# Attention's probabilities turned in 32x32 blocks by VectorE and put in place by DMA from SP's queue, instead of turned by TensorE; ten fillers at the beginning instead of eight

## Chip, cores, metric

The kernel runs on one core of a Trainium2 chip. The metric is the device time in microseconds of one execution. The version before took 2187.5 us (median of three runs, 2187.41 to 2187.93).

## What is computed

One decoder layer over 256 tokens of width 2048: a SwiGLU block with hidden width 5632, a mixer, a second SwiGLU block, each followed by a residual and a LayerNorm. The mixer projects the tokens by w_in, runs attention in nine pieces, gates the results and multiplies by two branch matrices and w_o. The change touches the part between scores and values:

```
proj = h @ w_in                                  # q, k, v of all branches, and the gates
# for each branch and group of four heads:
s = einsum('bhqd,bhkd->bhqk', q, k) * scale
p = exp(where(mask, s, -inf) - max)              # divided by its sum later
o = einsum('bhqk,bhkd->bhqd', p, v)
...
merged = sigmoid(g_a) * (o_nsa @ w_branch_a) + sigmoid(g_b) * (o_dil @ w_branch_b)
mix = merged @ w_o
```

Queries lie along the partitions after the scores. The values' product contracts over the keys, so the probabilities must be turned: keys along the partitions.

## The kernel before

**Weights in slots.** Every weight matrix goes through the core in 776 slots of two 128-row blocks by 512 columns (512 KB). SP loads a slot into one of four buffers `raw` (`load_slot`, L491), ScalarE rounds it to `w_hi` (`round_slot`, L519), VectorE writes the remainder `w_lo` (`split_slot`, L526), TensorE multiplies (`multiply_slot`): eight 128x512 matmuls with `w_hi` (L536, L537) and four with `w_lo` (L542). `w_hi` and `w_lo` have four buffers each too. SP may load a slot once the slot four before it is split, and ScalarE may round it once TensorE has used the slot four before it.

**The mixer's order.** The mixer has 192 slots (`MIX_SEQ`). Slots 32 to 79 are a mixture: behind each two slots of w_in stands one slot of the compression's weights (`cmp_slot`), which has two matmuls with `w_hi` (L1955) and two with `w_lo` (L1958) only, so it is short. Every third slot from 34 to 79 is such, slots 58, 61, 64 and 76 among them. `plan()` gives each small task of attention a slot behind which TensorE does it: turning queries and keys (`qT`, `kT`), scores (`s`, L1852, L1856, L1847), turning probabilities (`pT`, L1874), values (`pv`, L1905). ScalarE and VectorE take a task's result out of its PSUM bank two slots later in their own order (`LAG`). All engines' orders are written out from this table.

**Nine units.** `UNITS` 0 to 3 are selected and window attention of the two groups, 4 and 5 the compressed one, 6 to 8 the three dilated patterns. Units 0 to 3 and 6 have three blocks of 512 columns (four heads by 128 keys), units 7 and 8 two: 19 blocks in seven units. Each block is turned by four transposes on TensorE (`probs_T`, L1874, a matmul with the identity) into a PSUM bank, and VectorE copies it to `pT` (L1532). Before the scores of unit u+1 are masked into the same buffers (`mask_scores`, L1319), VectorE waits until TensorE has turned unit u's last block.

**Where the units stand.** In unit 0 the turns are at slots 58 to 60, the next scores at 61 to 63, the values at 65 and 66; in unit 1 at 71 to 73, 74 to 76, and 78 and 79.

**A form of the same technique** is there already: in both SwiGLU blocks the hidden activations are turned in 32x32 blocks by VectorE (`turn_blocks`, L1096), and 16 DMAs of ScalarE's queue put the blocks in place in `hT_lo` (`place_h`, L725), 256 pieces of 128 bytes each.

**The beginning.** Before the first weights are there, TensorE does `WARM_START` matmuls of zeros (`keep_warm`, L1642), then the first chunk (L1664, L1667, L1671).

Of the kernel before, what the change touches and what calls it, by code (L numbers as in the profile page):

```python
# [23 lines left out]
F32 = mybir.dt.float32  # L24
# [5 lines left out]
P = 128  # L30
# [17 lines left out]
WARM_START = 8  # L48
# [85 lines left out]
class Plan:  # L134


    def __init__(self):
        self.k, self.uses, self.t, self.at, self.by_pos = 1, [1, 1, 0, 0], {}, {}, {}
        self.turn = list(range(BANKS))

# [8 lines left out]
def plan():  # L149
# [36 lines left out]
    for u, (kind, g, ready) in enumerate(UNITS):  # L186
# [15 lines left out]
        n_probs = n_blocks(u)  # L202
        earliest = max(scored + 8, pv_read - 1)
        for j in range(n_probs):
            earliest = place(("pT", u, j), earliest)
        probs_read = earliest
        earliest += 5
# [51 lines left out]
def build(nc, x, xT_c, vec_c, w1_gate, w1_up, w1_down, ln1_g, ln1_b, w_in, ck_w2, cv_w2, ckv_w1,  # L259
# [9 lines left out]
    with ctx:  # L269
# [70 lines left out]
        s0 = sb("s0", [P, HPG, P])  # L340
        s1 = sb("s1", [P, HPG, TOKENS])
# [3 lines left out]
        pT = sb("pT", [P, 3, HPG, P])  # L345
# [68 lines left out]
        h_split = sem("h_split")  # L414
        var_ready = sem("var_ready")
# [286 lines left out]
        def exponentials(act, u, heads):  # L702
# [8 lines left out]
            for e in heads:  # L711
                v = s0[:, e] if e < HPG else s1[:, e - HPG, 0:P] if by_class(u) else s1[:, e - HPG]
                nc.scalar.activation(v, v, ACT.Exp, bias=negmax[:, u, e:e + 1], scale=SCALE,  # L713
                                     accum_out=sums[:, u, e:e + 1]).then_inc(probs_ready, 1)

        def place_h(act, f, i, n):
# [3 lines left out]
            for v in range(2 * (n - PLACE_FROM), 2 * (n - PLACE_FROM) + 2):  # L720
# [4 lines left out]
                act.dma_start(dst, src).then_inc(h_placed[f], 16)  # L725

# [12 lines left out]
        def _(sp):  # L739
# [311 lines left out]
        def _(dve):  # L1051
# [242 lines left out]
            def mask_scores(name, t):  # L1294
# [4 lines left out]
                if u:  # L1299
                    last = max(T[("pT", u - 1, jj)].k for jj in range(n_blocks(u - 1)))  # L1300
                    dve.wait_ge(bank_filled, last + 1)
                m = 0 if kind != DIL else 1 + g
# [4 lines left out]
                elif by_class(u):  # L1307
                    src = bank[:, t.bank, :].rearrange("p (h n) -> p h n", h=HPG)
                    dst = s0[:, :, :] if j == 0 else s1[:, :, 0:P]
# [11 lines left out]
            def maxima(u):  # L1321
# [10 lines left out]
                link(nc.vector.tensor_reduce(negmax[:, u, HPG:2 * HPG], s1[:, :, 0:P] if by_class(u) else s1[:, :, :], AX_X, ALU.max))  # L1332
                nc.vector.tensor_scalar(negmax[:, u, :], negmax[:, u, :], -SCALE, None, ALU.mult).then_inc(max_ready, 1)  # L1333

# [123 lines left out]
            for pos in range(MIX_SLOTS):  # L1458
# [56 lines left out]
                for name in pl.by_pos.get(pos - LAG, ()):  # L1515
# [3 lines left out]
                    elif name[0] == "pT":  # L1519
# [4 lines left out]
                        if UNITS[u][0] == CMP:  # L1524
                            n = HPG * N_CMP
                            hi, lo = pT_cmp[0:n, j, :], pT_cmp[V_ROW:V_ROW + n, j, :]
                            link(nc.vector.memset(pT_cmp[V_ROW // 2:V_ROW, j, :].bitcast(F32), 0.0))
                            link(nc.vector.tensor_copy(hi, bank[0:n, t.bank, 0:P]))
                            nc.vector.tensor_tensor(lo, bank[0:n, t.bank, 0:P], hi.bitcast(F32), ALU.subtract) \
                                .then_inc(bank_emptied[t.bank], 1)  # L1530
                        else:
                            nc.vector.tensor_copy(pT[:, j], bank[:, t.bank, :].rearrange("p (h n) -> p h n", h=HPG)) \  # L1532
                                .then_inc(bank_emptied[t.bank], 1)
# [16 lines left out]
                if pos in max_at:  # L1550
                    maxima(max_at[pos])
                if pos - 2 in max_at and UNITS[max_at[pos - 2]][0] == CMP:
# [69 lines left out]
        def _(pe):  # L1622
# [237 lines left out]
            def probs_T(name, t):  # L1860
# [4 lines left out]
                if UNITS[u][0] == CMP:  # L1865
                    n = HPG * N_CMP
                    mm = nc.tensor.transpose(bank[0:n, t.bank, 0:P], s0[:, 0, 0:TILES * HPG * N_CMP][:, j * n:(j + 1) * n], ident)
                else:
                    for h in range(HPG):
                        if by_class(u):  # L1870
                            v = s1[:, h, 0:P] if j else s0[:, h, :]
                        else:
# [196 lines left out]
```

## Time and profile before

| | |
|---|---|
| median of three runs | 2187.5 us |
| profiled execution, its own time | 2188.59 us |
| its span, first to last instruction | 2186.8 us |
| mean granted TensorE clock | 0.998 |
| TensorE busy | 2174.1 us, 99% of the span |
| VectorE busy | 1265.2 us, 58% |
| ScalarE busy | 964.6 us, 44% |
| DMA queue 1 (SP's), share of 16 engines | 63.2% |
| mixer's slots 30 to 190 in the trace | about 817 to 1294 us |

A row of a timeline gives start and duration in us, the engine, line, operation, tiles written and read, and how often it is repeated; in brackets, idle time before it and what ended it. PE is TensorE, DVE VectorE, ACT ScalarE; SPq and ACTq are DMAs issued by SP and ScalarE. Ends of matmuls are modelled, so the distance between two starts is what one costs. A 128x128 matmul in float32 shows as two records.

### The profile page before, as it was taken

What the parts mean: (1) busy time and instruction counts of PE and PEld (TensorE: products, weight loads), DVE (VectorE), ACT (ScalarE), POOL (GpSimd) and SP (SyncE); (2) the same over time, 40 slices, a digit from 0 to 9 for tenths busy, and PEclk for the clock granted to TensorE, in tenths of its full rate; (3) what the DMA queues carried; (4) which work ended last, traced back from release to release, by engine and by line L of the source; (5) the groups of instructions that cost most, each with busy time, mean ns of one, the idle gap of its engine ahead of it and who ended that gap; (6) DMA issues with size and microseconds to landing.
All of it is one profiled execution on the core that took longest, in us unless ns stands there. A gap on an engine that the chain in (4) does not pass through costs nothing.

```text
span 2186.8 us, 26659 instructions
## 1 busy us (share of the span) xinstructions
PE 2174.1 (99%) x9852; PEld 1801.2 (82%) x9852; DVE 1265.2 (58%) x1238; ACT 964.6 (44%) x1097; POOL 7.7 (0%) x12
## 2 busy tenths in 40 slices
PE   9999999999999999999999999999999999999998
PEld 8888888888888888888888888888888888888886
DVE  5555555554444767776655646567555555555445
ACT  5444444444333645544354444464444444444332
POOL 0000000000000000000000000000000000000000
PEclk9999999999999999999999999999999999999999
DMA  8767676777566666756567576656767676776664
GB/s 291 217 194 214 193 218 191 218 233 210 194 193 193 179 197 194 218 166 171 157 181 202 166 222 200 191 167 201 216 196 217 191 216 198 212 244 195 193 193 139
DMA packets 316203, 436.50 MB, mean 200 GB/s; under 512 B 112096, under 2 KB 112864, under 8 KB 315104
## 3 DMA queue, kind: packets, MB, share of 16 engines
q1 hardware_dynamic: 220096, 423.38, 63.2%
q10 hardware_dynamic: 96032, 12.08, 3.5%
q8 instruction: 51, 0.84, 0.2%
q14 instruction: 24, 0.20, 0.0%
HBM read 420.18 MB, written 3.68 MB: 194 GB/s over the span
## 4 chain that ended last, share of the span: by engine, by line
PE 99%; DVE 0%; ACT 0%; DMA 0%; DVEq 0%; issue 0%
PE acc L536 31%; PE acc L537 31%; PE acc L542 31%; PE bank L1905 1%; PE acc L1664 1%; PE acc L1667 1%; PE acc L1671 1%; PE bank L575 0%; PE bank L1745 0%; PE bank L1852 0%; PE bank L1874 0%; PE bank L1958 0%; PE bank L1955 0%; PE bank L1856 0%; PE bank L1847 0%; PE bank L1631 0%
## 5 line engine op out<-in xcount | busy, mean ns | idle before, releaser
L526 DVE TENSOR_TENSOR w_lo<-raw,w_hi 128x1024 fp32r<-128x1024 f32 x768 | 931.9, 1224 | 621.9 <-ACT w_hi L519 618.5
L519 ACT ACTIVATE w_hi<-raw 128x1024 fp32r<-128x1024 f32 x766 | 805.5, 1059 | 911.0 <-PE acc L542 815.6
L536 PE MATMUL acc<-w_hi,act_hi 128*128 128x512 f32 x2160 | 851.6, 394 | 0.0
L537 PE MATMUL acc<-w_hi,act_lo 128*128 128x512 f32 x2160 | 842.4, 390 | 0.0
L542 PE MATMUL acc<-w_lo,act_hi 128*128 128x512 f32 x2160 | 579.6, 390 | 0.0
L542 PEld LDWEIGHTS acc<-w_lo,act_hi 128*128 128x128 f32 x2160 | 405.5, 188 | 85.5 <-DVE w_lo L526 0.9
L536 PEld LDWEIGHTS acc<-w_hi,act_hi 128*128 128x128 f32 x2160 | 405.8, 188 | 83.8 <-issue 1.0
L537 PEld LDWEIGHTS acc<-w_hi,act_lo 128*128 128x128 f32 x2160 | 406.2, 188 | 81.6
L537 PE MATMUL acc<-w_hi,hT_lo 128*128 128x512 f32 x688 | 267.9, 389 | 0.0
L536 PE MATMUL acc<-w_hi,hT_hi 128*128 128x512 f32 x688 | 267.9, 389 | 0.0
L542 PE MATMUL acc<-w_lo,hT_hi 128*128 128x512 f32 x688 | 185.2, 389 | 0.0
L537 PEld LDWEIGHTS acc<-w_hi,hT_lo 128*128 128x128 f32 x688 | 129.3, 188 | 26.7
L542 PEld LDWEIGHTS acc<-w_lo,hT_hi 128*128 128x128 f32 x688 | 129.2, 188 | 26.7
L536 PEld LDWEIGHTS acc<-w_hi,hT_hi 128*128 128x128 f32 x688 | 129.2, 188 | 26.7
L1083 DVE SCALAR_TENSOR_TENSOR gate_t<-gate_t,acc 128x1024 f32<-128x1024 f32 x22 | 26.9, 1222 | 91.7 <-ACT gate_t L868 91.7
L868 ACT ACTIVATE gate_t<-acc 128x1024 f32<-128x1024 f32 x22 | 22.6, 1028 | 95.0 <-PE acc L542 90.6
L1091 DVE TENSOR_TENSOR gate_t<-gate_t,acc 128x1024 f32<-128x1024 f32 x22 | 26.9, 1222 | 62.0 <-PE acc L542 59.4
L536 PE MATMUL acc<-w_hi,oT_hi 128*128 128x512 f32 x96 | 38.0, 396 | 0.0
L537 PE MATMUL acc<-w_hi,oT_lo 128*128 128x512 f32 x96 | 37.5, 390 | 0.0
L713 ACT ACTIVATE s<-s,negmax 128x128 f32<-128x128 f32 (+1 forms) x56 | 23.8, 428 | 20.3 <-DVE negmax L1333 20.3
L696 ACT ACTIVATE qT<-bank 128x512 f32<-128x512 f32 x14 | 10.4, 743 | 42.8 <-PE bank L1745 42.8
L1096 DVE STREAM_TRANSPOSE hid<-gate_t 128x1024 f32<-128x1024 f32 x22 | 27.3, 1239 | 0.0
(241 smaller groups left out, 866.1 us busy)
## 6 DMA issues: line engine op xcount, KB each, us to landing
raw<-in_ffn_w_down_dram SPq DMA_DIRECT2D x176, 512.0 KB, 4.6
raw<-in_w_in_dram SPq DMA_DIRECT2D x176, 512.0 KB, 3.9
raw<-in_ffn_w_gate_dram SPq DMA_DIRECT2D x175, 512.0 KB, 4.5
raw<-in_ffn_w_up_dram SPq DMA_DIRECT2D x175, 512.0 KB, 4.5
raw<-in_w_o_dram SPq DMA_DIRECT2D x32, 512.0 KB, 4.7
hT_lo<-hid ACTq DMA_DIRECT2D x352, 32.0 KB, 3.5
raw<-in_cmp_kv_w_dram SPq DMA_DIRECT2D x16, 512.0 KB, 4.1
raw<-in_w_branch_a_dram SPq DMA_DIRECT2D x16, 512.0 KB, 5.3
```

The costliest lines, as they stand in the source:

```text
L519: nc.scalar.activation(weights(n0, s if isinstance(i, int) and i == 0 else s + per)[0], raw[:, r, :], ACT.Copy).then_inc(hi_done, 1)
L526: nc.vector.tensor_tensor(lo, raw[:, r, :], hi.bitcast(F32), ALU.subtract).then_inc(lo_done, 1)
L536: nc.tensor.matmul(o, a_hi[:, kt0 + k, at], hi, start=first and k == 0, stop=False)
L537: nc.tensor.matmul(o, a_lo[:, kt0 + k, at], hi, start=False, stop=False)
L542: mm = nc.tensor.matmul(o, a_hi[:, kt0 + k, at], lo, start=False, stop=last and k == SLOT_KT - 1)
L713: nc.scalar.activation(v, v, ACT.Exp, bias=negmax[:, u, e:e + 1], scale=SCALE, accum_out=sums[:, u, e:e + 1]).then_inc(probs_ready, 1)
L868: nc.scalar.activation(gate_t[:, :, :], acc_pair(0), ACT.Tanh, scale=0.5).then_inc(gate_tanh, 1)
L1083: nc.vector.scalar_tensor_tensor(gate_t[:, :, :], gate_t[:, :, :], 1.0, acc_pair(0), ALU.add, ALU.mult).then_inc(acc_emptied[0], 1)
L1091: nc.vector.tensor_tensor(gate_t[:, :, :], gate_t[:, :, :], acc_pair(1), ALU.mult).then_inc(acc_emptied[1], 1)
L1096: nc.vector.transpose(hid_kt.rearrange("p k t n -> p t k n"), gate_t[:, :, :].rearrange("p t (k n) -> p t k n", n=P)) \
L1664: nc.tensor.matmul(o, act_hi[:, 2 * s + k, at], hi, start=s == 0 and k == 0, stop=False)
L1667: nc.tensor.matmul(o, act_lo[:, 2 * s + k, at], hi, start=False, stop=False)
```

## The change

- `s0` and `s1` become parts of one tile `probs`, 12 blocks of 128 columns (8 used in units 7 and 8). `pT` gets the same form.
- For the seven units that are not compressed, `pT` tasks leave TensorE's table. VectorE turns `probs` in place in two instructions (`turn_probs`), at the slots `pl.turned[u]` (56, 68, 80, 92, 130, 142, 154) and the one behind.
- SP issues 16 DMAs per unit (`place_probs`), four behind each of the loads of slots turned+7 to turned+10. Each moves 32 partitions by 12 (or 8) pieces of 128 bytes from `probs` to `pT`.
- VectorE's first mask of the next unit waits until all 16 have landed, and so does TensorE's first values task (at turned+8). With that, in unit 0 the next scores stay at slots 61 to 63 and the values stand at 64 and 65; in unit 1 the scores stand at 73 to 75 and the values at 76 and 77. Later tasks shift by up to four slots.
- `WARM_START` goes from 8 to 10.

```diff
-WARM_START = 8
+WARM_START = 10
...
+        else:
+            pl.turned[u] = max(scored + (6 if u == 0 else 5), pv_read)
+            probs_read = pl.turned[u] + 6
+            earliest = pl.turned[u] + 8
...
-        s0 = sb("s0", [P, HPG, P])
-        s1 = sb("s1", [P, HPG, TOKENS])
+        probs = sb("probs", [P, 3 * HPG, P])
+        s0 = probs[:, 0:HPG]
+        s1 = probs[:, HPG:].rearrange("p (h j) n -> p h (j n)", h=HPG)
...
+        def place_probs(eng, u, moves):
+
+            eng.wait_ge(probs_turned, 2 * turned_to(u))
+            if u:
+                wait_filled(eng, T[("pv", u - 1, 1)])
+            n = HPG * (2 if by_class(u) else 3)
+            for v in moves:
+                b, q = divmod(v, QUADS)
+                src = probs[QUAD * b:QUAD * b + QUAD, 0:n].rearrange("p m (q j) -> p m q j", q=QUADS)[:, :, q, :]
+                dst = pT[QUAD * q:QUAD * q + QUAD, 0:n].rearrange("p m (b j) -> p m b j", b=QUADS)[:, :, b, :]
+                eng.dma_start(dst, src).then_inc(probs_placed, 16)
...
             for pos in range(MIX_SLOTS + TAIL_SLOTS):
                 load_slot(sp, mix_src[pos], mix_slot, 0, 0, pos)
+                for u in turned_units:
+                    k = pos - pl.turned[u] - 3 - RING
+                    if 0 <= k < 4:
+                        place_probs(sp, u, range(4 * k, 4 * k + 4))
...
                 wait_filled(dve, t)
-                if u:
+                if u and UNITS[u - 1][0] == CMP:
                     last = max(T[("pT", u - 1, jj)].k for jj in range(n_blocks(u - 1)))
                     dve.wait_ge(bank_filled, last + 1)
+                elif u:
+                    wait_placed(dve, u - 1)
...
+            def turn_probs(u, half):
+
+                dve.wait_ge(probs_ready, exps_before[u + 1])
+                n = HPG if by_class(u) else 6
+                v = probs[:, n * half:n * half + n].rearrange("p m n -> p (m n)")
+                nc.vector.transpose(v, v).then_inc(probs_turned, 1)
...
                 pe.wait_ge(probs_ready, exps_before[u + 1])
                 wait_bank_free(pe, t)
-                if UNITS[u][0] == CMP:
-                    n = HPG * N_CMP
-                    mm = nc.tensor.transpose(bank[0:n, t.bank, 0:P], s0[:, 0, 0:TILES * HPG * N_CMP][:, j * n:(j + 1) * n], ident)
-                else:
-                    for h in range(HPG):
-                        if by_class(u):
-                            v = s1[:, h, 0:P] if j else s0[:, h, :]
-                        else:
-                            v = s1[:, h, j * P:(j + 1) * P] if j < 2 else s0[:, h, :]
-                        mm = nc.tensor.transpose(bank[:, t.bank, h * P:(h + 1) * P], v, ident)
...
-                for j in range(n_blocks(u)):
-                    wait_moved(pe, T[("pT", u, j)])
+                if kind == CMP:
+                    for j in range(n_blocks(u)):
+                        wait_moved(pe, T[("pT", u, j)])
+                else:
+                    wait_placed(pe, u)
```

The order on VectorE around unit 0, before. L526 is a split; L1412 to L1420 work on keys and queries of a finished chunk; L1532 copies a turned block; L1319 masks a block of unit 1's scores.

```order
L526 TENSOR_TENSOR w_lo<-raw,w_hi 128x1024
L1417 TENSOR_TENSOR chunks_lo<-acc,rope 128x1024
L526 TENSOR_TENSOR w_lo<-raw,w_hi 128x1024
L1420 TENSOR_TENSOR chunks_lo<-chunks_lo,rot_tmp 128x1024
L526 TENSOR_TENSOR w_lo<-raw,w_hi 128x1024 x2
L1532 COPY pT<-bank 128x512
L526 TENSOR_TENSOR w_lo<-raw,w_hi 128x1024
L1532 COPY pT<-bank 128x512
L526 TENSOR_TENSOR w_lo<-raw,w_hi 128x1024
L1532 COPY pT<-bank 128x512
L526 TENSOR_TENSOR w_lo<-raw,w_hi 128x1024
L1319 TENSOR_TENSOR s<-bank,masks 128x512
```

The same place now (L535 is the split, L1378 a turn, L1357 the mask):

```order
L1378 STREAM_TRANSPOSE probs<-probs 128x768
L535 TENSOR_TENSOR w_lo<-raw,w_hi 128x1024
L1462 TENSOR_TENSOR chunks_lo<-acc,rope 128x1024
L1378 STREAM_TRANSPOSE probs<-probs 128x768
L535 TENSOR_TENSOR w_lo<-raw,w_hi 128x1024
L1465 TENSOR_TENSOR chunks_lo<-chunks_lo,rot_tmp 128x1024
L535 TENSOR_TENSOR w_lo<-raw,w_hi 128x1024 x5
L1357 TENSOR_TENSOR probs<-bank,masks 128x512
L535 TENSOR_TENSOR w_lo<-raw,w_hi 128x1024
L1357 TENSOR_TENSOR probs<-bank,masks 128x512
```

The three copies between the splits are gone, two turns stand among the splits of slots 56 to 58, and the first mask stands behind five splits in a row.

The order on SP at the same unit, now; before, only the loads stand here. L500 is a load of weights, L757 the moves.

```order
L500 DMA raw<-in_w_in_dram 128x2x512 x2
L757 DMA pT<-probs 32x12x32 x4
L500 DMA raw<-in_cmp_kv_w_dram 128x2x512
L757 DMA pT<-probs 32x12x32 x4
L500 DMA raw<-in_w_in_dram 128x2x512
L757 DMA pT<-probs 32x12x32 x4
L500 DMA raw<-in_w_in_dram 128x2x512
L757 DMA pT<-probs 32x12x32 x4
L500 DMA raw<-in_cmp_kv_w_dram 128x2x512
```

Behind each of the loads of slots 63 to 66 stand four moves; the load of slot 67 follows the last.

## Rows read from the trace of the kernel before

**Rows 1.** The page, part 1: busy us, share of the span, instructions
```profile
PE 2174.1 (99%) x9852; PEld 1801.2 (82%) x9852; DVE 1265.2 (58%) x1238; ACT 964.6 (44%) x1097; POOL 7.7 (0%) x12
```
**Rows 2.** The page, part 4: chain that ended last, by engine
```profile
PE 99%; DVE 0%; ACT 0%; DMA 0%; DVEq 0%; issue 0%
```
**Rows 3.** Timeline of TensorE, 918 to 925 us: two slots and two turned blocks
```profile
918.45 0.39 PE L536 MATMUL acc<-w_hi,act_hi 128*128 128x512 f32 x1
...
921.18 0.60 PE L1874 MATMUL bank<-small,s 128*128 128x128 f32 x4
921.54 0.48 PE L536 MATMUL acc<-w_hi,act_hi 128*128 128x512 f32 x1
...
924.39 0.60 PE L1874 MATMUL bank<-small,s 128*128 128x128 f32 x4
```
**Rows 4.** VectorE's groups by line: count, busy us, mean ns, idle before and releaser
```profile
L526 DVE TENSOR_TENSOR w_lo<-raw,w_hi 128x1024 fp32r<-128x1024 f32 x768 | 931.9, 1224 | 621.9 <-ACT w_hi L519 618.5 <-ACT w_hi L879 1.1
L1096 DVE STREAM_TRANSPOSE hid<-gate_t 128x1024 f32<-128x1024 f32 x22 | 27.3, 1239 | 0.0
...
L1319 DVE TENSOR_TENSOR s<-bank,masks 128x512 f32<-128x512 f32 x19 | 13.1, 692 | 23.7 <-PE bank L1847 8.8 <-PE bank L1852 8.6 <-PE bank L1856 6.2
L1532 DVE COPY pT<-bank 128x512 f32<-128x512 f32 x19 | 13.1, 690 | 17.7 <-PE bank L1874 17.7
```
**Rows 5.** Timeline of VectorE around unit 0: splits of slots 56, 59 and 60, 64
```profile
877.58 1.22 DVE L526 TENSOR_TENSOR w_lo<-raw,w_hi 128x1024 fp32r<-128x1024 f32 x1 [1.69 <-ACT w_hi L519]
...
884.58 2.35 DVE L526 TENSOR_TENSOR w_lo<-raw,w_hi 128x1024 fp32r<-128x1024 f32 x2
...
894.69 1.22 DVE L526 TENSOR_TENSOR w_lo<-raw,w_hi 128x1024 fp32r<-128x1024 f32 x1
```
**Rows 6.** Timeline of SP: load of slot 63; short DMAs of other tiles in a row
```profile
885.83 0.37 SPq L491 DMA_DIRECT2D raw<-in_w_in_dram  x1
...
1155.59 0.60 SPq L835 DMA_DIRECT2D negmax<-stats_by_token  x1
1156.24 0.61 SPq L835 DMA_DIRECT2D sums<-stats_by_token  x1
```
**Rows 7.** Tile hT_lo: issue ns min/median/max, and landing us
```profile
L725 ACTq DMA_DIRECT2D hT_lo<-hid x352: 613/615/1196, 54.7 to 1959.2; - x176
...
DMA to landing us min/median/max: 1.9/3.5/6.0
```
**Rows 8.** The page, part 3: queue of ScalarE: packets, MB, share of 16 engines
```profile
q10 hardware_dynamic: 96032, 12.08, 3.5%
```
**Rows 9.** The page, part 6: w_in's loads, KB each, median us to landing
```profile
raw<-in_w_in_dram SPq DMA_DIRECT2D x176, 512.0 KB, 3.9
```
**Rows 10.** Timeline of TensorE at slots 64 and 76, both of the compression
```profile
901.63 0.63 PE L1958 MATMUL bank<-w_lo,blk_both 128*124 128x512 f32 x2
...
933.92 0.64 PE L1958 MATMUL bank<-w_lo,blk_both 128*124 128x512 f32 x2
```
**Rows 11.** Who waited for whom: us in total, times, longest
```profile
ACT w_hi L519 <- PE acc L542: 815.6, 530, 3.5
...
ACT w_hi L519 <- DMA raw<-in_w_in_dram: 33.1, 20, 3.4
```
**Rows 12.** Timeline of the first 16 us
```profile
1.06 3.78 PE L1642 MATMUL bank<-hid 128*128 128x128 f32 x16 [1.06 <-DVE ln_s L1281]
...
5.52 1.22 PE L1664 MATMUL acc<-w_hi,act_hi 128*128 128x512 f32 x2 [0.68 <-ACT w_hi L877]
...
6.21 1.23 DVE L526 TENSOR_TENSOR w_lo<-raw,w_hi 128x1024 fp32r<-128x1024 f32 x1 [0.65 <-ACT w_hi L879]
...
7.88 1.22 DVE L526 TENSOR_TENSOR w_lo<-raw,w_hi 128x1024 fp32r<-128x1024 f32 x1 [0.45 <-ACT w_hi L879]
...
9.10 1.11 PE L1671 MATMUL acc<-w_lo,act_hi 128*128 128x512 f32 x4
...
10.54 2.55 DVE L526 TENSOR_TENSOR w_lo<-raw,w_hi 128x1024 fp32r<-128x1024 f32 x2 [0.83 <-ACT w_hi L519]
```

More of the change, by code:

```diff
@@ L139, in __init__ @@
         self.turn = list(range(BANKS))
+        self.turned = {}
 class Task:
@@ L201, in plan @@
         scored = earliest
[L202 to L207, printed above, removed]
+        if kind == CMP:
+            earliest = max(scored + 8, pv_read - 1)
+            for j in range(n_blocks(u)):
+                earliest = place(("pT", u, j), earliest)
+            probs_read = earliest
+            earliest += 5
+        else:
+            pl.turned[u] = max(scored + (6 if u == 0 else 5), pv_read)
+            probs_read = pl.turned[u] + 6
+            earliest = pl.turned[u] + 8
         for tile in range(TILES):
@@ L711, in exponentials @@
             for e in heads:
-                v = s0[:, e] if e < HPG else s1[:, e - HPG, 0:P] if by_class(u) else s1[:, e - HPG]
+                v = s0[:, e] if e < HPG else s1_class[:, e - HPG] if by_class(u) else s1[:, e - HPG]
                 nc.scalar.activation(v, v, ACT.Exp, bias=negmax[:, u, e:e + 1], scale=SCALE,
@@ L725, in place_h, with turned_to, wait_placed @@
                 act.dma_start(dst, src).then_inc(h_placed[f], 16)
+        turned_units = [u for u in range(len(UNITS)) if UNITS[u][0] != CMP]
+        n_moves = QUADS * QUADS
+        def turned_to(u):
+            return sum(v <= u for v in turned_units)
+        def wait_placed(eng, u):
+            eng.wait_ge(probs_placed, 16 * n_moves * turned_to(u))
+        def place_probs(eng, u, moves):
[8 more added lines that the diff above has]
+                eng.dma_start(dst, src).then_inc(probs_placed, 16)
         out_t = out[0].rearrange("(t p) d -> p t d", p=P)
@@ L1308, in mask_scores @@
                     src = bank[:, t.bank, :].rearrange("p (h n) -> p h n", h=HPG)
-                    dst = s0[:, :, :] if j == 0 else s1[:, :, 0:P]
+                    dst = s0[:, :, :] if j == 0 else s1_class
                     msk = masks[:, 2, (g - 1) * P:g * P].unsqueeze(1).broadcast_to([P, HPG, P])
@@ L1551, in _ @@
                     maxima(max_at[pos])
+                for u in turned_units:
+                    if pos in (pl.turned[u], pl.turned[u] + 1):
+                        turn_probs(u, pos - pl.turned[u])
                 if pos - 2 in max_at and UNITS[max_at[pos - 2]][0] == CMP:
@@ L1864, in probs_T, with probs_T_block @@
                 wait_bank_free(pe, t)
[L1865 to L1875 removed]
+                n = HPG * N_CMP
+                nc.tensor.transpose(bank[0:n, t.bank, 0:P], s0[:, 0, 0:TILES * HPG * N_CMP][:, j * n:(j + 1) * n], ident) \
+                    .then_inc(bank_filled, 1)
+            def probs_T_block(u, j, h):
+                if by_class(u):
+                    return pT[:, HPG * j + h, :]
+                return pT[:, h if j == 2 else HPG + 2 * h + j, :]
             def values(name, t):
@@ L1879, in values @@
                 kind, g, _ = UNITS[u]
-                for j in range(n_blocks(u)):
-                    wait_moved(pe, T[("pT", u, j)])
+                if kind == CMP:
+                    for j in range(n_blocks(u)):
+                        wait_moved(pe, T[("pT", u, j)])
+                else:
+                    wait_placed(pe, u)
                 if kind == CMP:
@@ L1904, in values @@
                     for n, (j, kt) in enumerate(parts):
-                        mm = nc.tensor.matmul(o, pT[:, j, h, :], v[:, kt, c0:c0 + HEAD], start=n == 0,
+                        mm = nc.tensor.matmul(o, probs_T_block(u, j, h), v[:, kt, c0:c0 + HEAD], start=n == 0,
                                               stop=n == len(parts) - 1)
```

21 lines of the change are left out of this document (11 added, 10 removed).

## The prediction

> **What bounds the kernel now.** I read the page's first part, then its chain, then TensorE's timeline in the mixer, then who waits. TensorE is busy for 2174.1 us of the 2186.8 us span [rows 1], and 99% of the chain that ended last is TensorE [rows 2]. So only two things count: time that an instruction takes on TensorE, and new idle time in front of one. In the mixer TensorE does one slot of w_in after another and puts one small task of attention behind a slot. A slot of twelve 128x512 matmuls takes 2.73 us (918.45 to 921.18). Four turns of probabilities then take 0.36 us (921.18 to 921.54), and the slot behind them takes 2.85 us, 0.12 us more than one with nothing before it [rows 3]. VectorE and ScalarE have idle time in that stretch; VectorE alone waited 618.5 us for ScalarE [rows 4]. Neither bounds the end, as long as w_lo is ready when TensorE asks.
>
> **The profiled execution.** It took 2188.59 us, 1.8 us above its span and 1.1 us above the median of 2187.5 us. The sum below is a difference; I put it on the median. Two programs of this kernel can be told apart from about 0.2%, 4.4 us.
>
> **Part 1, the turns leave TensorE.** They go with nothing in their place on this engine: 19 blocks (the 19 copies of L1532 count them [rows 4]) of four. Each is worth 0.36 + 0.12 = 0.48 us, so **-9.1 us**. In front of one of the short slots (compression, four matmuls) the after-effect is 0.08 us and not 0.12; that would take 0.1 us off the sum. No task is put in between, and no slot waits longer for a bank because of it.
>
> **Part 2, VectorE.** 19 copies of 0.69 us go [rows 4], 13.1 us. There come ten turns of 128x768 and four of 128x512. The row of the same instruction is 1.24 us for 1024 columns [rows 4], so 0.93 and 0.62 us, 11.8 us in all. In sum nothing, and VectorE is not the bound. But the place differs: the copies stood where VectorE waited for TensorE, the two turns of a unit stand some six slots earlier, and for unit 0 that is a stretch in which VectorE has no gap from 877.58 us until behind 884.58 us [rows 5]. So slots 57 to 60 are split 1.85 us later there, and with them come the loads of slots that wait for a free raw buffer.
>
> **Part 3, the train on SP's queue.** Each unit gets 16 moves, four behind each of four loads. SP begins a 0.60 us issue of this kind every 0.65 us [rows 6]; the moves that ScalarE's queue does now for hT_lo take 0.615 us of issue [rows 7]. I take 0.66 us a move (bounds: 0.42 us, which is a load's issue with its gap, and 0.75 us), so a group of one load and four moves takes 0.42 + 4 x 0.66 = 3.06 us. The last of the 16 starts 3 x 3.06 + 0.42 + 3 x 0.66 = 11.6 us after the first load does.
> Its landing: an hT_lo move takes 1.9 us at the least, 3.5 us in the median, 6.0 us at most [rows 7]. Its 128-byte packets are cheap: queue 10 moved 96,032 in 3.5% of 16 x 2186.8 us, 12.8 ns each [rows 8]; a move of 384 takes 24 x 12.8 ns = 0.3 us of each of 16 engines. A load of w_in lands 3.9 us after issue [rows 9], and I take it that the four moves land behind it, 0.3 us apart: 3.9 + 1.2 = 5.1 us after the last load, which starts 2.4 us before the last move. That is 2.7 us after the last move's own issue, between 1.9 and 4.6 us.
>
> **Part 4, the new wait.** Unit u+1's first mask overwrites what the moves read, so it waits for all 16. Behind it on VectorE stands the split of the very slot behind which TensorE multiplies unit u's values. Unit 0: load 63 starts at 885.83 us [rows 6], 1.85 us later by part 2, 887.7 us; last move 899.3 us; landed 902.0 us; mask 0.69 and split 1.22 us less their overlap of 0.1: w_lo of slot 64 is there at 903.8 us. TensorE wants it at 901.63 us [rows 10], 1.44 us earlier with three blocks gone: 900.2 us. It stands for **3.6 us**. Without the later start and with the soonest landing it would be 0.9 us; with the slowest issue and landing, 7 us.
> Unit 1 is laid the same: slot 76 is a short one too, with only two matmuls ahead of its w_lo part at 933.92 us [rows 10], where a full slot has eight, 1.8 us. I take 3.0 us there, since part of the lateness is shared by both ends. Units 2, 6 and 7 have a full slot at that place, and the loads are less dense: I take nothing, with 0 to 2 us each as bounds. A last 0.5 us is for unit 1's own turns, which stand between dense splits. Stalls in all: **+7.1 us** (bounds 1 and 20). The values' own wait hides behind this one: the moves have landed before.
> The loads that follow a group start up to 5 us later than now. What covers this is the lead of the split weights: slot 64's w_lo ends at 895.9 us [rows 5] for a use at 901.63 us [rows 10], 5.7 us; and in most slots ScalarE waits for TensorE and not for the load: 530 waits for the one, 20 for w_in's loads [rows 11]. With 5 us of lateness it is just enough, and this is the thinnest cover in the argument.
>
> **Part 5, ten fillers.** The eight fillers are 16 passes from 1.06 us [rows 12], the last starts 0.42 us before 4.84, and the first real matmul starts at 5.52 us after 0.68 us of idle time. Two more are 4 passes of 0.21 us: they end at about 5.5 us and cost 0 to 0.1 us. What can they give? Matmuls of 512 columns start 0.43 us apart up to 9.10 us and 0.23 us apart from there [rows 12]: 1.2 GHz, then 2.4 GHz, though the engine was busy from 5.52 us on, and before that idle time from 1.06 us on. If the idle time is what kept the clock down, eight matmuls run at the higher level, 8 x 0.2 = 1.6 us. w_lo of the first slot is ready at 7.44 us and of the next at 9.10 us, VectorE is at the third and fourth from 10.54 us on [rows 12]; so the data allow about 1.5 us. I take **-1.5 us** (bounds 0.1 and -1.9).
>
> **Sum.** -9.1 + 7.1 - 1.5 = -3.5 us: 2187.5 - 3.5 = **2184.0 us**.
>
> **The rivals.**
> A, the moves are in time. If SP issues a move as fast as a load (0.42 us), a group takes 2.1 us and the last move starts 3 x 2.1 + 4 x 0.42 = 8.0 us after the first load; from 887.7 us on that puts w_lo of slot 64 at 887.7 + 8.0 + 2.7 + 1.8 = 900.2 us, just when TensorE asks. For it: the loads of the same queue take 0.37 us [rows 6]. Against: every issue with few partitions took 0.52 to 0.61 us. Time: 2187.5 - 9.1 - 1.5 = 2176.9 us. Chance 0.22.
> B, slower: the moves clog SP's ring. They share it with the loads, where those of hT_lo have a ring of their own, and those still took up to 6.0 us. If a move takes 0.6 us of the engines behind the load instead of 0.3 us, a group takes 1.4 + 2.4 = 3.8 us, the train 3 us more, the loads behind are late as well; 7 us each in units 0 and 1, and some 2 us in each of units 2, 6 and 7: 20 us. Time: 2187.5 - 9.1 + 20 - 1.5 = 2196.9 us. It decides from 0.45 us a move on, since stalls above 10.6 us outweigh both gains. Chance 0.13.
> The Trainium skill speaks for B: in DMA: Bandwidth & Descriptors, section Measured (HBM→SBUF, 128 partitions, SWDGE, issued from GpSimd), transfers below 64 KB are dominated by descriptors, and 64 KB takes 0.95 us. By that figure, an estimate, a group would take 1.4 + 3.8 = 5.2 us, and the time would be above B's. The row of 12.8 ns a packet speaks against it.
> C, the fillers give nothing, the rest as forecast: 2185.5 us. Chance 0.15.
> D, the edit does not do what it says: excluded, in the built order no turn of probabilities but compression's is left on TensorE, and nothing else there is longer.
>
> **How the numbers follow.** Forecast 0.50, A 0.22, C 0.15, B 0.13. Faster by more than 0.2% is below 2183.1 us: all of A, 0.4 of the forecast, none of B and C: 0.42. Slower by more than 0.2% is above 2191.9 us: most of B, 0.11. Within: 0.47. The range reaches from A, 2176.5 us, to a stall of 15 us, 2191.5 us, and leaves out half of A's lower side and most of B.
>
> **What would show it.** On TensorE two idle gaps of about 3 us before the compression slots' w_lo matmuls (slots 64 and 76), released by VectorE, and none of note elsewhere in the mixer. On VectorE, before the first masks of units 1 and 2, idle times of 6 to 8 us released by the DMA of pT. On SP, moves 0.66 us apart in trains of 11.6 us. L1874's place on TensorE gone, slots behind it at 2.73 us. At the start, fillers up to 5.5 us and the pace of 0.23 us some 3 us earlier. The prediction is wrong if there are no such gaps (A), if moves land more than 6 us after issue or full slots wait for w_hi (B), or if the pace changes at 9.1 us as before (C).

## The result, and the profile after

| | before | changed |
|---|---|---|
| median | 2187.57 us (18 runs) | 2191.22 us (17 runs) |
| profiled execution, its span | 2188.59, 2186.8 us | 2190.58, 2188.8 us |
| ratio of changed to before, 95% interval | | 1.0017 (1.0010 to 1.0023) |

The change makes the kernel 3.7 us slower; the forecast was 3.5 us faster. (Two executions with a much lower mean granted clock are left out, here and below: one of the changed kernel, 2407.69 us at 0.849, and one of the kernel before, 3683.35 us at 0.555.)

First the page of the changed kernel: what the engines did, and the chain, as in [rows 1, 2].

```profile
PE 2168.5 (99%) x9780; PEld 1794.5 (82%) x9780; DVE 1263.2 (58%) x1233; ACT 964.4 (44%) x1097; POOL 7.7 (0%) x12
...
PE 94%; DVE 2%; SPq 2%; ACT 1%; DMA 1%; issue 0%; DVEq 0%; ACTq 0%
```

TensorE has 72 instructions less (76 turns gone, which show as one record each; four filler passes more) and is busy 5.6 us less, yet the span is 2 us longer. The chain, 99% TensorE before, now goes through VectorE, SP's queue and a DMA. Where, the windows say; the columns are the stretch, its length, busy time of each engine with its instructions, the granted clock of TensorE, the DMA share and GB/s. The first row is the kernel before, the others are the changed one:

```profile
860.00:1000.00 140.00, 140.00 (x703) 117.92 (x702) 100.76 (x123) 67.17 (x122) 0.00 (x0) 1.00 0.65 191
...
860.00:1000.00 140.00, 132.32 (x628) 110.22 (x627) 97.19 (x119) 64.91 (x116) 0.00 (x0) 0.98 0.74 197
1000.00:1200.00 200.00, 199.50 (x974) 165.08 (x973) 117.98 (x143) 90.73 (x138) 0.00 (x0) 1.00 0.70 189
```

TensorE is idle 7.7 us between 860 and 1000 us and 0.5 us between 1000 and 1200 us; before, it was never idle in either. And the clock of the first stretch is 0.98, which matters below. Who waits there (all waits of the changed kernel, total, times, longest):

```profile
DVE probs L1357 <- DMA pT<-probs: 33.5, 5, 9.0
...
PEld bank L2003 <- DVE w_lo L535: 9.3, 4, 4.3
PE bank L2003 <- DVE w_lo L535: 7.7, 3, 3.8
```

That is the chain forecast in part 4: the mask (L1357) waits for the moves, the split behind it is late, and L2003, the w_lo part of a compression slot, waits for the split. The timeline around slot 64 of unit 0, all engines but the weight loads:

```profile
886.32 3.31 SPq L757 DMA_DIRECT2D pT<-probs  x4
889.68 0.61 SPq L500 DMA_DIRECT2D raw<-in_cmp_kv_w_dram  x1
890.33 2.58 SPq L757 DMA_DIRECT2D pT<-probs  x4
892.95 0.61 SPq L500 DMA_DIRECT2D raw<-in_w_in_dram  x1
893.61 2.58 SPq L757 DMA_DIRECT2D pT<-probs  x4
896.23 0.62 SPq L500 DMA_DIRECT2D raw<-in_w_in_dram  x1
896.90 2.58 SPq L757 DMA_DIRECT2D pT<-probs  x4
...
898.73 0.71 PE L2000 MATMUL bank<-w_hi,blk_both 128*124 128x512 f32 x2
...
901.38 0.69 DVE L1357 TENSOR_TENSOR probs<-bank,masks 128x512 f32<-128x512 f32 x1 [8.97 <-DMA pT<-probs]
901.99 1.22 DVE L535 TENSOR_TENSOR w_lo<-raw,w_hi 128x1024 fp32r<-128x1024 f32 x1
...
903.26 1.21 PE L2003 MATMUL bank<-w_lo,blk_both 128*124 128x512 f32 x2 [3.83 <-DVE w_lo L535]
...
904.27 1.91 PE L1950 MATMUL bank<-chunks_lo,pT 128*128 128x128 f32 x8
```

The last four moves are issued from 896.90 to 899.48 us, the mask starts at 901.38 us, the split takes 1.22 us, and TensorE has been idle for 3.83 us. The same stands at slot 76 of unit 1:

```profile
936.25 0.71 PE L2000 MATMUL bank<-w_hi,blk_both 128*124 128x512 f32 x2
940.44 1.21 PE L2003 MATMUL bank<-w_lo,blk_both 128*124 128x512 f32 x2 [3.49 <-DVE w_lo L535]
941.45 1.91 PE L1950 MATMUL bank<-chunks_lo,pT 128*128 128x128 f32 x8
```

The last row of both pieces has something the forecast lacks. Eight values' matmuls take 1.91 us from first start to last end; nearly everywhere else they take 1.05 us. The windows behind the two waits show why (granted clock in the third column from the right):

```profile
903.20:906.40 3.20, 3.14 (x12) 2.87 (x13) 3.03 (x6) 0.00 (x0) 0.00 (x0) 0.51 0.61 163
...
940.40:943.60 3.20, 3.16 (x12) 2.87 (x13) 3.03 (x5) 0.00 (x0) 0.00 (x0) 0.51 0.60 164
```

For 3.2 us behind each of these two waits TensorE was granted 0.51 of its clock, the lower of its two levels (1.2 GHz); at the higher level the same work would take 1.6 us. So each of them costs 1.6 us more than its idle time.

### The profile page after: what moved, and what is told of

Read it like the earlier page. It is cut to its first block, busy times and chain, and to the rows that moved or that the text cites. A ratio compares the mean times of both kernels' runs of the same rounds, so it can differ in the third digit from the quotient of the medians.

```text
span 2188.8 us, 26597 instructions
## 1 busy us (share of the span) xinstructions
PE 2168.5 (99%) x9780; PEld 1794.5 (82%) x9780; DVE 1263.2 (58%) x1233; ACT 964.4 (44%) x1097; POOL 7.7 (0%) x12
## 2 busy tenths in 40 slices
DMA packets 356907, 441.48 MB, mean 202 GB/s; under 512 B 152800, under 2 KB 153568, under 8 KB 355808
## 4 chain that ended last, share of the span: by engine, by line
PE 94%; DVE 2%; SPq 2%; ACT 1%; DMA 1%; issue 0%; DVEq 0%; ACTq 0%
PE acc L545 30%; PE acc L546 30%; PE acc L551 30%; SPq L757 1%; DVE w_lo L535 1%; PE acc L1715 1%; PE acc L1708 1%; PE acc L1711 1%; PE bank L1950 1%; PE bank L584 0%; ACT probs L722 0%; PE bank L1789 0%; DMA pT<-probs 0%; ACT w_hi L528 0%; PE bank L1896 0%
## 5 line engine op out<-in xcount | busy, mean ns | idle before, releaser
L535 DVE TENSOR_TENSOR w_lo<-raw,w_hi 128x1024 fp32r<-128x1024 f32 x768 | 931.2, 1224 | 631.9 <-ACT w_hi L528 627.9
L722 ACT ACTIVATE probs<-probs,negmax 128x128 f32<-128x128 f32 (+1 forms) x56 | 23.9, 428 | 32.0 <-DVE negmax L1371 32.0
L1357 DVE TENSOR_TENSOR probs<-bank,masks 128x512 f32<-128x512 f32 x19 | 13.1, 689 | 42.1 <-DMA pT<-probs 33.5
```

The source lines that it names most:

```text
L535: nc.vector.tensor_tensor(lo, raw[:, r, :], hi.bitcast(F32), ALU.subtract).then_inc(lo_done, 1)
```

## The experiments

Medians in one table; each row's ratio is against runs of the kernel before on the same chip in the same batch (its median 2187.1 us for e1 to e4, 2187.51 us for e5 to e8, 2187.22 us for e9 to e12).

| | kernel | median, us | ratio, 95% interval |
|---|---|---|---|
| e1 | before, ten fillers | 2187.57 | 1.0000 (0.9991 to 1.0010) |
| e2 | moves one slot sooner | 2184.44 | 0.9986 (0.9977 to 0.9996) |
| e3 | moves two slots sooner | 2183.72 | 0.9985 (0.9976 to 0.9994) |
| e4 | fillers in the waits, own bank | 2192.56 | 1.0024 (1.0015 to 1.0033) |
| e5 | before, again | 2186.87 (one) | |
| e6 | zeros added in the waits | 2190.50 | 1.0012 (1.0003 to 1.0021) |
| e7 | units 0 and 1 on TensorE | 2181.16 | 0.9969 (0.9957 to 0.9981) |
| e8 | moves on two queues | 2180.64 | 0.9967 (0.9955 to 0.9979) |
| e9 | e8, ScalarE's a slot later | 2179.22 | 0.9964 (0.9950 to 0.9978) |
| e10 | e9 with eight fillers | 2179.56 | 0.9964 (0.9951 to 0.9978) |
| e11 | all moves on ScalarE's queue | 2186.73 | 0.9996 (0.9987 to 1.0005) |
| e12 | units 0 and 1 alone by DMA | 2195.95 | 1.0039 (1.0026 to 1.0053) |

### e1, the fillers by themselves

```diff
 (the kernel before)
-WARM_START = 8
+WARM_START = 10
```

> The kernel before with ten fillers and nothing else. In the changed kernel the idle time of 0.68 us ahead of the first real matmul is gone, and matmuls start 0.23 us apart from 5.90 us on instead of 9.10 us; the events behind the start stand 1.7 us earlier. Theory: that is the work of the two added fillers alone, so 1.7 us less than before, 2185.9 us. Rival: the earlier start is an accident of this profile, or is given back; then 2187.5 us.

2187.57 us against 2187.1 us: the gain is not there. Yet its profile does show the fast pace early, from 6.35 us on. The runs of the kernel before explain it: over all four batches there are 82, 62 at 2186.7 to 2188.2 us and 20 at 2188.6 to 2189.4 us. The profile read for the prediction, 2188.59 us, belongs to the upper 20. That called for a second profile. (None of e1's 11 runs lies in the upper group, the highest is 2188.50 us. With one in four there, that would be chance about once in twenty, so ten fillers may keep the slow executions away. That is not shown, and the median has nothing of it.)

### e5, the kernel before, profiled again

No edit.

> The kernel before, unchanged, for a second profile. In the runs so far its times fall into two groups, 38 of 50 at 2186.7 to 2188.2 us and 12 at 2188.7 to 2189.4 us, and the profile read for the prediction (2188.59 us) is of the upper one; the kernel with ten fillers has no such upper group and gained nothing in the median. Theory: in most runs of the kernel before the pace of 0.23 us begins as early as with ten fillers (at 6 us instead of 9.10 us), in spite of the 0.68 us of idle time; a profile of a run at about 2187.0 us shows that. Rival: the pace changes at 9.1 us in both groups, and what the fillers win is lost behind the start.

2186.87 us. The start on TensorE of this second execution of the same program, to be held against [rows 12]:

```profile
1.06 3.78 PE L1642 MATMUL bank<-hid 128*128 128x128 f32 x16 [1.06 <-DVE ln_s L1281]
5.29 0.72 PE L1664 MATMUL acc<-w_hi,act_hi 128*128 128x512 f32 x2 [0.44 <-ACT w_hi L877]
5.85 0.63 PE L1667 MATMUL acc<-w_hi,act_lo 128*128 128x512 f32 x2
```

A pair takes 0.62 us, which is two matmuls 0.23 us apart, from 5.85 us on, with eight fillers and with idle time in front of the first real matmul. The changed kernel does the same:

```profile
1.06 4.46 PE L1686 MATMUL bank<-hid 128*128 128x128 f32 x20 [1.06 <-DVE ln_s L1317]
5.34 0.72 PE L1708 MATMUL acc<-w_hi,act_hi 128*128 128x512 f32 x2
5.90 0.63 PE L1711 MATMUL acc<-w_hi,act_lo 128*128 128x512 f32 x2
```

So the late rise of the clock in [rows 12] is how this execution went, not how the program goes, and it is in the profile that the sum was made from. Little else tells the two executions of the kernel before apart: at VectorE's twelfth split the first is 1.8 us behind the second, and at the last, 2125 us later, 1.7 us. Only one profile of each group was taken; that every run of the upper group starts slowly is likely (the distance of the groups, 1.7 us between their medians, is that of the two profiles) and not shown. The Trainium skill, TensorE: Matmul & The Clock Gate, section What's actually happening, says that the number of slow matmuls at a kernel's start differs from run to run of one kernel; these two profiles agree.

From here on e5 is the base: the last matmul starts at 2173.95 us in it and at 2177.69 us in the changed kernel, 3.7 us later, as much as the medians differ. All of it comes in the mixer: VectorE's splits before it are 0.1 us apart in the two profiles, those behind it 3.7 us. The times in [rows 5, 6, 10] are some 1.7 us later than those of the same instructions in e5.

### e2 and e3, the moves sooner

```diff
-                    k = pos - pl.turned[u] - 3 - RING
+                    k = pos - pl.turned[u] - 2 - RING      (e2)
+                    k = pos - pl.turned[u] - 1 - RING      (e3)
```

> The changed kernel with each group of four moves behind the load of one slot earlier (3.3 us sooner). Theory: the two long waits in slots 64 and 76 (3.83 and 3.49 us of idle time) shrink to 0.5 us or less each, and with them goes the half clock behind each (0.51 of full for 3.2 us, 1.6 us lost): -3.3 - 3.3 - 3.2 = -9.8 us, so 2181.5 us. Rival 1: the half clock behind the waits comes from something else than the idle time (the DMA traffic, the kind of matmul), and stays: 2184.7 us. Rival 2: the moves are held up by the loads in the same ring and land no sooner: 2191 us.

> The same two slots earlier; SP now waits behind load 61 until VectorE has turned the second half (load issued at 880.5 us, turned at 882.5 us), and the loads behind it are held. Theory: both waits are gone whole and the loads have enough lead; 0.5 to 1 us below the kernel with one slot, 2180.5 us. Rival: the held loads come late for ScalarE (landed only as it starts, in slots 58 to 64), and new gaps of 1 to 3 us appear in front of w_hi: 2183 to 2186 us.

e2: 2184.44 us, 6.8 us below the changed kernel; forecast were 9.8. Its slot 64:

```profile
899.98 0.69 DVE L1357 TENSOR_TENSOR probs<-bank,masks 128x512 f32<-128x512 f32 x1 [6.17 <-DMA pT<-probs]
...
901.86 0.73 PE L2003 MATMUL bank<-w_lo,blk_both 128*124 128x512 f32 x2 [1.99 <-DVE w_lo L535]
902.42 1.05 PE L1950 MATMUL bank<-chunks_lo,pT 128*128 128x128 f32 x8
```

The idle time is 1.99 us, not 0.5, since the train starts only 1.9 us sooner (first move at 884.4 us against 886.3 us), behind a load that still waits for its buffer. But the eight values take 1.05 us: behind this shorter wait the clock is whole (granted 1.00 from 901.8 to 905 us), and both half clocks are gone. Both parts of the rival fall here: these are the same matmuls, and the DMA engines are busier than behind the changed kernel's wait (share 0.98 against 0.61). e3 gives another 0.7 us, as forecast about, though the ranges of the two kernels overlap; its largest gap left is 1.84 us between matmul starts, at 917 us, and w_hi is late at two places, by 0.45 and 0.78 us. Taking moves sooner alone does not clear the way.

### e4 and e6, TensorE kept busy in the wait

```diff
                     nc.tensor.matmul(o, both, b_hi[:, cs], start=s == 0 and k == 0, stop=False)
+                t = warm_at.get(n - mix_slot)              (e4; slots 64 and 76)
+                if t:
+                    wait_bank_free(pe, t)
+                    for _ in range(14):
+                        nc.tensor.matmul(bank[0:KV_ROWS, t.bank, :], steps[0][0], b_hi[:, 0:COLS], start=True, stop=True)
+                if n - mix_slot in warm_at:                (e6)
+                    pe.wait_ge(zero_ready, 1)
+                    for _ in range(14):
+                        nc.tensor.matmul(o, steps[0][0], zero[:, :], start=False, stop=False)
```

> The changed kernel, its moves where they are, with 14 matmuls of 512 columns (3.2 us at 0.23 us each) put into each of the two waits, in front of slot 64's and slot 76's w_lo part; their results are overwritten. The wait for VectorE stays as long. Theory: the clock falls because TensorE is idle for 3.5 to 3.8 us; kept busy, it does the w_lo matmuls 0.23 us and the eight values 0.112 us apart (now 0.213 us), which gives 1.6 us in each place: 2191.3 - 3.2 = 2188.1 us. Rival: the half pace has another cause, and the time stays at 2191.3 us or more.

> The changed kernel with 14 matmuls of 512 columns in front of slot 64's and slot 76's w_lo part that multiply the slot's stationary block by zeros and add that to the open sum (3.2 us at 0.23 us each); they wait for nothing but a memset long done. The wait for VectorE itself stays. Theory: idle time of 3.5 to 3.8 us is what lowers the clock; with it cut to 0.6 us the eight values behind start 0.112 us apart (now 0.213 us), and 1.6 us is given back in each place: 2191.3 - 3.2 = 2188.1 us. Rival: the half pace belongs to the DMA traffic or the kind of matmul and stays: 2191.3 us.

e4 was badly made for slot 64: the bank that its matmuls write into is freed by the very mask that waits.

```profile
903.06 5.06 PE L2007 MATMUL bank<-w_hi,blk_both 128*124 128x512 f32 x14 [3.12 <-DVE probs L1357]
```

They came behind 3.12 us of idle time and took 5.06 us instead of 3.4, so there they only added to the time. It shows by accident that quite other matmuls behind an idle time run slowly too, though here the granted clock was 1.00 for the first 1.6 us and 0.50 for the next 3.2 us. In slot 76 the same matmuls came behind 1.39 us, took 3.53 us, and no half clock followed.

e6 has the edit right (it fills `zero` once, at the beginning). Slots 64 and 76 of e6, and the granted clock behind them:

```profile
899.31 3.40 PE L2009 MATMUL bank<-zero,blk_both 128*124 128x512 f32 x14
904.35 0.73 PE L2012 MATMUL bank<-w_lo,blk_both 128*124 128x512 f32 x2 [1.64 <-DVE w_lo L537]
904.91 1.05 PE L1953 MATMUL bank<-chunks_lo,pT 128*128 128x128 f32 x8
...
937.89 3.42 PE L2009 MATMUL bank<-zero,blk_both 128*124 128x512 f32 x14
941.33 0.72 PE L2012 MATMUL bank<-w_lo,blk_both 128*124 128x512 f32 x2
```

```profile
904.30:907.50 3.20, 3.15 (x18) 2.76 (x19) 3.03 (x5) 0.00 (x0) 0.00 (x0) 1.00 0.59 161
941.30:944.50 3.20, 3.18 (x19) 2.79 (x19) 3.03 (x5) 0.00 (x0) 0.00 (x0) 1.00 0.62 163
```

The wait for VectorE is as long as before, the transfers are the same, and the clock stays whole: idle TensorE is the cause of the half clock, shown. The gain is not what was expected, 0.7 us instead of 3.2. In this profile the mask chain of slot 64 ended 1.1 us later, because SP took 4.37 us to issue the first four moves and not 3.31, and further on new gaps stand where the changed kernel has none: 1.7 us between starts at 920.6 us and 0.9 us at 950.7 us. What the clock gave back was lost again where loads and splits came late, in this one profile; that it is so in every run is not shown.

### e7 and e12, units 0 and 1 apart

```diff
+def by_dma(u):
+    return UNITS[u][0] != CMP and u > 1                    (e7; e12: u < 2)
...
-        if kind == CMP:
+        if not by_dma(u):
             earliest = max(scored + 8, pv_read - 1)
```

and the same test wherever the changed kernel asks for a compression unit, with the turns and copies of the kernel before for the other units.

> The changed kernel with units 0 and 1 turned by TensorE as before, the other seven turned units' work (units 2, 3, 6, 7 and 8) through VectorE and DMA. Theory: the stalls and the half clock behind them belong to units 0 and 1, whose first mask stands in front of the split of a short slot; 13 of 19 blocks stay off TensorE, at 0.46 us each (8.7 us for 19 in the two profiles) -6.0 us, some 0.5 us stays in unit 7: 2187.3 - 5.5 = 2181.8 us. Rival: units 2 and 3 take over the stall, since their loads are the next to be late: 2186 us or more.

> The changed kernel with units 0 and 1 alone turned by VectorE and DMA, and units 2, 3, 6, 7 and 8 by TensorE: the other half of the kernel in which these two were left on TensorE. Theory: the parts add up: 6 of 19 blocks give -2.7 us, the waits of units 0 and 1 with their half clocks cost the most of 12.4 us, 11.9 us: 2187.3 - 2.7 + 11.9 = 2196.5 us. Rival: part of that wait is lateness that the loads regain behind it when the later units need no moves: 2193 to 2195 us.

(Five units stay with the DMA in e7; "seven" is a slip in the text.) e7 takes 2181.16 us, e12 2195.95 us: both within 0.7 us of their forecasts, e12 in part by luck, as below. The rivals fall: units 2 and 3 do not inherit the stall, and later loads do not make it good. e7 still has VectorE waiting 17.5 us for the moves at three masks, and no gap on TensorE in the mixer: a wait of VectorE with a full slot behind it is hidden. Against 2187.3 us, the median of all 82 runs of the kernel before, the two halves make -6.1 and +8.7 us, together +2.6, where the whole makes +3.9. In e12 the second wait was shorter:

```profile
941.00 0.72 PE L2021 MATMUL bank<-w_lo,blk_both 128*124 128x512 f32 x2 [2.53 <-DVE w_lo L540]
941.57 1.05 PE L1968 MATMUL bank<-chunks_lo,pT 128*128 128x128 f32 x8
```

2.53 us of idle time, and no half clock behind it. But behind the first wait, 3.52 us, the half clock lasted twice as long as in the changed kernel:

```profile
903.50:909.90 6.40, 6.38 (x20) 5.39 (x21) 6.13 (x10) 1.79 (x9) 0.00 (x0) 0.52 0.60 164
```

That is 3.1 us lost behind one wait, as much as behind the changed kernel's two. So 1.6 us is not a fixed price of a stall, and e12's forecast, which took two half clocks of 1.6 us, was met by luck in that term.

### e8, e9 and e11, which queue

```diff
             (SP, behind its loads; e8 and e9)
-                    k = pos - pl.turned[u] - 3 - RING
-                    if 0 <= k < 4:
+                    k = pos - pl.turned[u] - 2 - RING
+                    if 0 <= k < 2:
                         place_probs(sp, u, range(4 * k, 4 * k + 4))
             (ScalarE, behind its w_hi)
+                for u in turned_units:
+                    k = pos - pl.turned[u] - 2             (e8; e9: - 3)
+                    if 0 <= k < 4:
+                        place_probs(act, u, range(8 + 2 * k, 10 + 2 * k))
```

e11 has no moves on SP, and on ScalarE's queue, with - 3, `range(4 * k, 4 * k + 4)`.

> The changed kernel with eight of the 16 moves on SP's queue, four behind each of two loads and one slot earlier, and eight on ScalarE's queue, two in each of four slots from the turning on. Theory: the wait is the length of the train on one queue (13.2 us from first to last move, paced by the loads); halved, the last move starts 6.6 us sooner than now, both stalls and the half clocks go, and all 19 blocks count: 2187.3 - 8.7 + 0.5 = 2179.1 us. Rival: what takes the time is the DMA engines, which serve loads and moves alike; then the moves land as late as in the kernel one slot earlier, 2184.4 us, and ScalarE loses 1.2 us a slot that it cannot spare, so 2185 us or more.

> The kernel with two queues, ScalarE's moves one slot later (from the second slot behind the turning on). In the profile of the kernel with two queues ScalarE stood 5.52 us at its first two moves, waiting for the second turning, then rounded w_hi of slot 58 late, and TensorE had 0.8 us of idle time before that slot's successor and 0.6 us at the same place of unit 1. Theory: these go, -1 to -1.5 us, 2179.4 us. Rival: the last moves are now late for the mask (landing 3.3 us later) and a wait of VectorE comes back in front of slot 64: 2181 to 2183 us.

> The changed kernel with all 16 moves on ScalarE's queue, four in each of four slots from the second behind the turning on, and none on SP's. Theory: the length of the train on one queue makes the wait, whichever queue it is: ScalarE gives 1.06 us to w_hi and 2.6 us to four moves in each slot, 3.7 us against SP's 3.3 us a group, so the last move starts as late as in the changed kernel, both waits and the half clocks stay, and w_hi comes late besides: 2191 us or more. Rival: SP's ring, shared with loads of 512 KB, is what delays the moves; on a queue without loads they are issued faster and land sooner, 2182 us.

e8, 2180.64 us: no wait for the moves is left, but ScalarE stands for the turning and is late with w_hi, as the expectation of e9 says. e9 mends that. Its slot 64, VectorE and then TensorE:

```profile
895.11 0.68 DVE L1361 TENSOR_TENSOR probs<-bank,masks 128x512 f32<-128x512 f32 x1
```

```profile
898.82 0.72 PE L2004 MATMUL bank<-w_hi,blk_both 128*124 128x512 f32 x2
899.38 0.62 PE L2007 MATMUL bank<-w_lo,blk_both 128*124 128x512 f32 x2
899.84 1.05 PE L1954 MATMUL bank<-chunks_lo,pT 128*128 128x128 f32 x8
```

The mask starts at 895.11 us without a wait, 6.3 us sooner, and TensorE goes through. At 2179.22 us **e9 beats both kernels**: 8.0 us below before, 12 us below the change. In its profile a single gap is left, 0.76 us between starts in slot 58, behind unit 0's own turns. The DMA packets are the same 356,907, so it was not the engines of the DMA that were short. The Trainium skill, DMA: Bandwidth & Descriptors, section Rules for kernel authors, says that spreading DMAs over SP and ScalarE adds no bandwidth and only saves issue time of the sequencers; the runs agree (357 thousand packets and 441 MB in both), and here the issue time is what set the wait.

e11 came out between its two texts, 2186.73 us. ScalarE's train:

```profile
883.79 2.63 ACTq L757 DMA_DIRECT2D pT<-probs  x4
...
886.55 2.65 ACTq L757 DMA_DIRECT2D pT<-probs  x4
...
889.33 4.56 ACTq L757 DMA_DIRECT2D pT<-probs  x4
...
894.01 3.09 ACTq L757 DMA_DIRECT2D pT<-probs  x4
```

It is 13.3 us long, where SP's is 13.2 us, and of that 12.9 and 11.1 us are the issues of the moves themselves: the length belongs to 16 moves on one queue, and the loads in SP's ring are not what makes it. (That the two lengths are so near is chance: between the groups stands a load on the one, a rounding on the other.) But it starts 2.5 us sooner, which shortens the mask's wait, and what is won is partly lost on w_hi, late at four places by 3.5 us in all. The expectation was wrong in taking equal length for equal end.

### e10, eight fillers again

```diff
-WARM_START = 10                                            (e9 with this edit)
+WARM_START = 8
```

> The same with eight fillers at the beginning, as in the kernel before. Theory: two fillers give nothing against the usual run (pace of 0.23 us from 5.85 us on with either number) and cost 0 to 0.5 us, so 2179.0 us, within 0.5 us of the kernel with ten, perhaps with some single runs 1.7 us above the rest. Rival: ten fillers give 1.5 us here, 2180.9 us.

2179.56 against 2179.22 us, five runs each, ranges that overlap: no difference. With e1 this makes two places where two more fillers change nothing that can be measured.

## Why the prediction was wrong

The forecast was 3.5 us faster, the kernel is 3.7 us slower, inside the range given (2176.5 to 2191.5 us). Two steps failed: part 4's price of a wait, by 3.2 us the larger, and part 5's gain, by 1.5 us. With both put right the sum is +1.2 us; the other 2.5 us are sizes, below.

**Part 1, the turns: right.** From e5 to e9 the last matmul moves from 2173.95 to 2165.98 us, 8.0 us; with the 0.5 us lost in slot 58 of e9, 8.5 us for 19 blocks, 0.45 us a block where 0.48 was forecast. e7, in whose mixer TensorE never stands, confirms it: from before the mixer to behind it VectorE's splits gain 6.0 us on e5's, 0.46 us for each of 13 blocks.

**Part 2: about right.** The groups of the turns:

```profile
L1378 DVE STREAM_TRANSPOSE probs<-probs 128x768 f32<-128x768 f32 x10 | 9.7, 972 | 0.1
L1378 DVE STREAM_TRANSPOSE probs<-probs 128x512 f32<-128x512 f32 x4 | 2.8, 704 | 0.0
```

12.5 us, forecast 11.8. The delay of the splits behind unit 0's turns costs 0.5 us in slot 58, in every kernel that turns unit 0 so; I had that half microsecond in unit 1.

**Part 3, the train: right in kind, short by a tenth.** A move is issued in 0.62 us in the median and lands 3.2 us after:

```profile
L757 SPq DMA_DIRECT2D pT<-probs x112: 591/620/1478, 886.3 to 1209.7; - x112
...
DMA to landing us min/median/max: 2.0/3.1/4.8
```

Groups are 3.3 us apart and not 3.06, because a load between moves takes 0.61 us to issue and not 0.37; the first four moves took 3.31 us and not 2.58 as the others. So the last move starts 12.9 us after the first load (forecast 11.6), and the mask starts 2.5 us after that (forecast 2.7). The forecast's times in the trace come from the profile with the slow start and have to be read 1.7 us earlier to be held against the changed kernel. In e5 the second of these two loads is that of slot 63:

```profile
881.87 2.64 SPq L491 DMA_DIRECT2D raw<-in_w_in_dram  x2
```

It starts at 884.1 us, in the changed kernel at 885.9 us: the delay of part 2, 1.8 us, is there. w_lo of slot 64 was forecast for 903.8, which is 902.1 us so read, and is there at 903.2 us.

**Part 4, the wait: right in place and idle time, wrong in price.** Forecast 3.6 and 3.0 us of idle time in slots 64 and 76, measured 3.83 and 3.49 (w_lo is 1.1 us later than forecast, and TensorE 0.8 us later there). VectorE's waits were forecast at 6 to 8 us and are 9.0 and 8.3. Missing is the term behind it, **half the clock for 3.2 us after each wait, 1.6 us each, 3.2 us in all**. The prediction counted a stall as its idle time alone. It had even the means: part 5 weighs idle time against the clock at the start, and never asks the same of the stalls that part 4 puts there. The Trainium skill, TensorE: Matmul & The Clock Gate, section HAM oscillation — how this bites in real kernels, describes just this, waits for data behind which TensorE runs cold again; the rows at 903.2 and 940.4 us agree (0.51). With the 3.2 us that these rows show the forecast would have been 0.3 us faster, no change.
The rest: unit 0's own turns and a late w_hi at 1189 us (0.5 us each). Part 4 says 7.1 us in all; what the changed kernel lost is 12.2 us, got by difference (8.5 + 3.7). All idle time makes 7.7 + 0.5 = 8.2 us of it, the half clock 3.2 us. Of the 0.8 us in neither most is in the same waits, which cost some 0.15 us more each from start to start than their idle time: in slot 64 there are 4.53 us from L2000 to L2003 where e9 has 0.56, so 3.97 against 3.83.

**Part 5, the fillers: the second step that failed, and outright.** -1.5 us was read from a profile whose start was the slow one, and put on a median whose runs mostly start fast. The prediction noted that this execution stood 1.1 us above the median and went on to treat the sum as a difference that does not care. It does, where the stretch costed is the one in which the executions differ. Against e5 the start gains nothing.

By the base e5: -8.5 + 12.2 + 0.0 = **+3.7 us**. In the forecast: -9.1 + 7.1 - 1.5 = -3.5.

**The rivals.** A (moves in time) is wrong for one queue, and is what e9 brings about with two: 2176.9 us forecast for it, 2179.2 us measured, the missing 1.5 us of the fillers included. B (the ring clogs, 20 us) is wrong: moves land 3.1 us after issue in the median, at most 4.8, and full slots hide VectorE's waits, as e7 shows. Its 1.4 us of the engines for a load is shown by no row; queue 1's share, 63.2% for 423 MB, makes it 1.7 us (estimate). The Trainium skill's figure of 0.95 us (DMA: Bandwidth & Descriptors, section Measured (HBM→SBUF, 128 partitions, SWDGE, issued from GpSimd)), of which the prediction made groups of 5.2 us, is not borne out for these moves: groups are 3.3 us apart. C (fillers give nothing) came true as to the fillers.

## What to carry to other kernels

Price a new wait on the busiest engine as its idle time and what the clock takes behind it (here nothing, 1.6 or 3.1 us), and read the second from a profile or, if there is none yet, carry it as an open term of the same order as the wait. Small moves that must all land before something else can go should be counted as a train, pieces times issue time, and spread over two issuing queues before their order is tuned. Before a gain is read from one profile, ask whether the runs of that kernel fall in groups, in which group the profile is, and take a second profile if it is above the median.

## What the runs showed of the hardware that was not expected

- Idle times of 3.12, 3.49, 3.52 and 3.83 us on TensorE (in e4, the changed kernel and e12) were each followed by work at half pace, and one such stretch in e12 was twice as long as the others (granted clock 0.52 over 6.4 us); those of 1.64, 1.99 and 2.53 us (in e6, e2 and e12) were not.
- 14 matmuls that add zeros kept the higher level through a wait and were worth 0.7 us, not 3.2: what they won was waited away behind them in the profile taken.
- An issue of a load on SP's queue takes 0.37 us by itself and 0.61 us between small moves:

```profile
880.52 0.37 SPq L500 DMA_DIRECT2D raw<-in_cmp_kv_w_dram  x1
```

- On ScalarE's queue single issues of a move took up to 2.1 us where four stood in a slot (median 0.64 us).
- One program had two starts: the pace of 0.23 us began at 9.10 us in one profile and at 5.85 us in the other.
